# The last expert's rows added from their row buffer, gathered rows by diagonal products, fillers at the entry

## The reference

```python
# hier_moe, cut
gate = softmax(top_v) * g_w                  # two experts of 32 for each token, with a weight each
def block(args):                             # rows of one expert
    tids, e, w = args
    xb = x_pad[tids]
    hdn = silu(xb @ w1[e]) * (xb @ w3[e])
    return (hdn @ w2[e]) * w[:, None]
out = segment_sum(y, slot_tok)               # each token adds its two rows
# after it, in both layers
x = layer_norm(DN_ALPHA * x + f, ln2_g[i], ln2_b[i])
```

## Time and profile before

| | |
|---|---|
| median of 3 runs | 2996.56 us (2993.69 to 2999.35) |
| profiled execution | 2994.94 us, span 2993.1 us |
| mean granted TensorE clock | 0.982 |
| TensorE busy | 2895.8 us, 97% of the span |
| VectorE busy | 2123.5 us, 71% |
| ScalarE busy | 1604.9 us, 54% |
| GpSimd busy | 358.4 us, 12% |
| memory read | 574.15 MB |

### The profile page before, as it was taken

The page is one execution under the profiler, slowest core; times in us unless marked ns, Lnnn a source line. Parts: engine busy times, 40 slices in busy tenths (PEclk is TensorE's granted clock), DMA queues, the critical chain, the costliest instruction groups (busy, mean ns, idle before and its releaser), DMA issues.

```text
span 2993.1 us, 38811 instructions
## 1 busy us (share of the span) xinstructions
PE 2895.8 (97%) x14261; PEld 2257.0 (75%) x14261; DVE 2123.5 (71%) x2376; ACT 1604.9 (54%) x1969; POOL 358.4 (12%) x273
## 2 busy tenths in 40 slices
PE   8999899999989999899999999999999999999998
PEld 7668776767768767677677668888888887888886
DVE  3485799999972467899999865674776648676762
ACT  3573588888853464788888743433222226522211
POOL 0000212222220002122222220100000000000000
PEclk9999899999999998999999999999999999999999
DMA  7303799999962125899999844301232223232222
GB/s 273 136 1 113 261 389 405 409 398 400 405 223 85 39 99 226 334 399 398 404 399 406 332 106 99 66 20 64 92 102 95 99 85 99 92 111 93 91 94 84
DMA packets 170900, 600.50 MB, mean 201 GB/s; under 512 B 21697, under 2 KB 71025, under 8 KB 121363
## 3 DMA queue, kind: packets, MB, share of 16 engines
q1 hardware_dynamic: 140432, 541.22, 48.5%
q0 software_dynamic: 19840, 52.60, 4.9%
q10 hardware_dynamic: 10499, 4.91, 0.6%
HBM read 574.15 MB, written 40.37 MB: 205 GB/s over the span
## 4 chain that ended last, share of the span: by engine, by line
PE 73%; DMA 11%; DVE 7%; ACT 5%; issue 3%; POOL 1%; DVEq 0%; SPq 0%; ACTq 0%; POOLq 0%
PE bank L2074 14%; PE bank L2076 14%; PE bank L2075 14%; DMA ring<-w_gate 6%; PE bank L2512 4%; PE bank L2509 4%; DMA ring<-w_up 3%; PE bank L2086 3%; PE bank L2794 2%; PE bank L2528 2%; PE bank L2081 2%; PE bank L2082 2%; PE bank L2138 1%; PE bank L2139 1%; ACT ring_rounded L1479 1%
## 5 line engine op out<-in xcount | busy, mean ns | idle before, releaser
L3601 DVE TENSOR_TENSOR ring_rounded<-ring,big_rounded 128x2048 fp32r<-128x2048 f32 x252 | 567.6, 2288 | 32.0 <-ACT big_rounded L1479 31.0
L1479 ACT ACTIVATE big_rounded<-ring 128x2048 fp32r<-128x2048 f32 x252 | 481.9, 1916 | 44.2 <-DMA ring<-w_up 33.2
L3096 DVE TENSOR_TENSOR ring_rounded<-ring,ring_rounded 128x2048 fp32r<-128x2048 f32 (+2 forms) x118 | 261.4, 2255 | 329.8 <-ACT ring_rounded L1221 329.4
L1221 ACT ACTIVATE ring_rounded<-ring 128x2048 fp32r<-128x2048 f32 (+2 forms) x124 | 226.5, 1876 | 369.3 <-DMA ring<-ffn_w_down 150.1
L3601 DVE TENSOR_TENSOR ring_rounded<-ring,ring_rounded 128x2048 fp32r<-128x2048 f32 x128 | 292.4, 2288 | 43.5 <-ACT ring_rounded L1479 43.1
L1479 ACT ACTIVATE ring_rounded<-ring 128x2048 fp32r<-128x2048 f32 x128 | 245.0, 1917 | 96.5 <-DMA ring<-w_gate 95.5
L2074 PE MATMUL bank<-XT_rounded,ring_rounded 128*128 128x512 f32 (+1 forms) x792 | 295.8, 374 | 0.4 <-DVE XH_rounded L3149 0.4
L2076 PE MATMUL bank<-XT_rounded,ring_rounded 128*128 128x512 f32 (+1 forms) x792 | 292.9, 370 | 0.0
L2075 PE MATMUL bank<-XH_rounded,ring_rounded 128*128 128x512 f32 (+1 forms) x792 | 292.9, 370 | 0.0
L2512 PE MATMUL bank<-ring_rounded,big_rounded 128*128 128x512 f32 x960 | 265.7, 399 | 7.4 <-DVE ring_rounded L3601 6.9
L2075 PE MATMUL bank<-ring_rounded,XH_rounded 128*64 128x512 f32 (+2 forms) x608 | 239.6, 394 | 0.0
(11 more groups left out here) (525 smaller groups left out, 5527.1 us busy)
## 6 DMA issues: line engine op xcount, KB each, us to landing
ring<-w_up SPq DMA_DIRECT2D x128, 1024.0 KB, 9.8
ring<-w_down SPq DMA_DIRECT2D x128, 1024.0 KB, 7.7
ring<-w_gate SPq DMA_DIRECT2D x128, 1024.0 KB, 7.9
ring<-ffn_w_up SPq DMA_DIRECT2D x44, 1024.0 KB, 7.0
ring<-ret_gdn_w_in SPq DMA_DIRECT2D x8, 2048.0 KB, 13.1
ring<-ffn_w_down SPq DMA_DIRECT2D x8, 2048.0 KB, 7.7
expert_rows<-lnp POOLq DMA_DIRECT2D x1, 12288.0 KB, 40.3
ring<-odd_w_qkv SPq DMA_DIRECT2D x6, 2048.0 KB, 8.1
```

Source lines behind the costliest of these rows:

```text
L1221: act.activation(one_pass(hi(c)[:, ks, :]), raw(c)[:, ks, :], ACT.Copy).then_inc(rounded[c.pair], 1)
L1479: act.activation(one_pass(expert_hi(j)), expert_raw(j), ACT.Copy).then_inc(signal("half_rounded").sem, 1)
L3096: dve.tensor_tensor(one_pass(w), w, parts(hi(c)[:, ks, :]), ALU.subtract).then_inc(split[c.pair], 1)
L3601: dve.tensor_tensor(one_pass(expert_raw(j)), expert_raw(j), parts(expert_hi(j)), ALU.subtract).then_inc(signal("half_split").sem, 1)
```

## The change

1. The last expert's rows aren't stored in the table and gathered again. VectorE builds, for each tile of tokens, a mark matrix (128 tokens x 64 places) that holds the token's gate weight at its place in the last expert's list. TensorE turns the four of them into one bank, ScalarE copies the result (`last_T`), and TensorE multiplies it with the row buffer.
2. The gathered rows are no longer added by VectorE. For each tile and each of the two choices VectorE makes a diagonal matrix of the token weights (`shares`), and TensorE multiplies it with the gathered rows into the same two banks. VectorE then only adds the banks to X.
3. GpSimd's gathers wait for 15 stores of the odd half and not 16, and for the last products that use the space of their targets.
4. Eight small VectorE operations (`last_weights`) come behind `gate_weights`, in front of expert 2.
5. In both layers two fillers go ahead of `positions(l, 0)` and two ahead of `positions(l, 1)`. The fillers at the seam fall from 9 to 0 after layer 0 and from 24 to 4 after layer 1.

All operands of the new products are plain f32.

```diff
@@ -1085,14 +1091,16 @@
                         pool.wait_ge(full[1], base[1] + e + 1)
                         gather(e + 2)
                 scatter(EXPERTS - 2)
-                scatter(EXPERTS - 1)
 
             def from_experts(l):
 
                 pool.wait_ge(signal("slots_ready").sem, signal("slots_ready").next(pool))
                 for half in range(2):
-                    pool.wait_ge(signal(f"y_stored{half}").sem, 16 * (EXPERTS // 2) * (l + 1))
+                    pool.wait_ge(signal(f"y_stored{half}").sem, 16 * (EXPERTS // 2 - half) * (l + 1))
+                pool.wait_ge(full[3], U[f"moe{l}"][3] + EXPERTS)
                 for t in range(T):
+                    if t == 2:
+                        pool.wait_ge(full[6], U[f"moe{l}"][6] + EXPERTS)
                     for j, dst in enumerate((XH[:, t, :], M["YG"][:, t, :])):
                         pool.indirect_dma_start(
                             dst, None, expert_rows, bass.IndirectOffsetOnAxis(ap=gath[:, TOP_K * t + j:TOP_K * t + j + 1], axis=0),
...
-            def moments(t):
-
-                act.wait_ge(signal("x_combined").sem, signal("x_combined").next(act))
+            def moments(l, t):
+
+                u = U[f"combined{l}"][2 * t + 1]
+                act.wait_ge(drained[u.bank], u.n + 1)
                 act.activation(XH[:, t, :], X[:, t, :], ACT.Copy, accum_out=ssq[:, 16 + t:17 + t]).then_inc(act_done.sem, 1)
...
+
+            def marks_T(l):
+
+                u = U[f"last{l}"]
+                act.wait_ge(full[u.bank], u.n + 1)
+                act.activation(M["last_T"], ps(u)[0:NARROW, :], ACT.Copy).then_inc(drained[u.bank], 1)
...
                 experts(0)
+                marks_T(0)
                 for c in W["qkv"][0:1]:
                     round_chunk(c)
...
@@ -2311,6 +2328,31 @@
 
                 return lambda t, kk: ap[:, kk, t * P:(t + 1) * P]
 
+            def marks_T(l):
+
+                u = U[f"last{l}"]
+                pe.wait_ge(signal("last_marked").sem, signal("last_marked").next(pe, T * (TOP_K + 1)))
+                pe.wait_ge(drained[u.bank], u.n)
+                for t in range(T):
+                    ins = pe.transpose(ps(u)[0:NARROW, t * P:(t + 1) * P], M["last"][:, t, :], ident)
+                ins.then_inc(full[u.bank], 1)
+
+            def combine(l, t):
+                base, u = U[f"moe{l}"], U[f"last{l}"]
+                if t == 0:
+                    pe.wait_ge(drained[u.bank], u.n + 1)
+                    for b in (5, 6):
+                        pe.wait_ge(drained[b], base[b] + EXPERTS)
+                us = U[f"combined{l}"][2 * t:2 * t + 2]
+                for c, v in enumerate(us):
+                    pe.wait_ge(drained[v.bank], v.n)
+                    pe.matmul(ps(v)[:, :], M["last_T"][:, t * P:(t + 1) * P], M["YE"][0:NARROW, 1, c * BANK:(c + 1) * BANK], start=True, stop=False)
+                pe.wait_ge(signal(f"rows_back{t}").sem, 16 * TOP_K * (l + 1))
+                for c, v in enumerate(us):
+                    for j, rows in enumerate((XH, M["YG"])):
+                        ins = pe.matmul(ps(v)[:, :], M["shares"][:, t, j, :], rows[:, t, c * BANK:(c + 1) * BANK], start=False, stop=(j == 1))
+                    ins.then_inc(full[v.bank], 1)
...
@@ -2445,9 +2487,13 @@
                 turn_tile(normed, X, 3, "x_normed")
                 logits(l, 2)
                 logits(l, 3)
-                for q in range(2):
-                    positions(l, q)
-                    first_rows(l, q)
+                spare = (4, 6)[l]
+                keep_warm(Use(spare, U[f"moe{l}"][spare]), 2)
+                positions(l, 0)
+                first_rows(l, 0)
+                keep_warm(Use(spare, U[f"moe{l}"][spare]), 2)
+                positions(l, 1)
+                first_rows(l, 1)
...
@@ -2711,9 +2757,12 @@
                 experts(0)
             if on(5):
                 pe.wait_ge(drained[U["rel"][0].bank], U["rel"][0].n + 1)
+                marks_T(0)
                 for j in range(EARLY_BIAS):
                     rel_bias(j)
-                first_chunk_by_tile("qkv", "ln20_T", X, "x_normed", feature_rows(x_lo_T), 9)
+                for t in range(T):
+                    combine(0, t)
+                first_chunk_by_tile("qkv", "ln20_T", X, "x_normed", feature_rows(x_lo_T), 0)
...
@@ -2734,7 +2783,11 @@
             if on(6):
                 experts(1)
             if on(7):
-                first_chunk_by_tile("mix_in", "rms0_T", XH, "xh_ready", None, 24)
+                marks_T(1)
+                keep_warm(U["combined1"][0], 4)
+                for t in range(T):
+                    combine(1, t)
+                first_chunk_by_tile("mix_in", "rms0_T", XH, "xh_ready", None, 0)
...
                 bounds(l)
                 gate_weights(l)
+                last_weights(l)
                 stage(2, 0, down=False)
...
-
-            def combine(t):
-
-                dve.wait_ge(signal(f"rows_back{t}").sem, signal(f"rows_back{t}").next(dve, 16 * TOP_K))
-                x = X[:, t, :]
-                dve.scalar_tensor_tensor(x, XH[:, t, :], wts[:, t, 0:1], x, ALU.mult, ALU.add).then_inc(dve_done.sem, 1)
-                dve.wait_ge(dve_done.sem, dve_done.next(dve))
-                dve.scalar_tensor_tensor(x, M["YG"][:, t, :], wts[:, t, 1:2], x, ALU.mult, ALU.add).then_inc(signal("x_combined").sem, 1)
-                dve.wait_ge(signal("x_combined").sem, signal("x_combined").next(dve))
+                last_marks(l)
+
+            def last_weights(l):
+
+                at, w, match, place_at = grp, gw, keep, wtmp
+                dve.tensor_scalar(n_most, which, float(EXPERTS - 1), float(2 - EXPERTS), ALU.is_equal, ALU.mult).then_inc(dve_done.sem, 1)
+                done()
+                dve.tensor_scalar(n_most, n_most, float(EXPERTS - 1), None, ALU.add).then_inc(dve_done.sem, 1)
+                done()
+                dve.tensor_scalar(match, ek, n_most, None, ALU.is_equal).then_inc(dve_done.sem, 1)
+                done()
+                dve.scalar_tensor_tensor(place_at, pos2, 1.0, match, ALU.add, ALU.mult).then_inc(dve_done.sem, 1)
+                done()
+                dve.scalar_tensor_tensor(at, place_at[:, :, 0], -1.0, place_at[:, :, 1], ALU.add, ALU.add).then_inc(dve_done.sem, 1)
+                done()
+                dve.tensor_tensor(match, match, wts, ALU.mult).then_inc(dve_done.sem, 1)
+                done()
+                dve.tensor_tensor(w, match[:, :, 0], match[:, :, 1], ALU.add).then_inc(dve_done.sem, 1)
+                done()
+                dve.tensor_tensor(wts, wts, match, ALU.subtract).then_inc(dve_done.sem, 1)
+                done()
+
+            def last_marks(l):
+
+                for t in range(T):
+                    dve.tensor_scalar(M["last"][:, t, :], k("places")[:, 0:NARROW], grp[:, t:t + 1], gw[:, t:t + 1], ALU.is_equal, ALU.mult).then_inc(
+                        signal("last_marked").sem, 1)
+                for t in range(T):
+                    for j in range(TOP_K):
+                        dve.tensor_scalar(M["shares"][:, t, j, :], ident, wts[:, t, j:j + 1], None, ALU.mult).then_inc(signal("last_marked").sem, 1)
+
+            def combine(l, t):
+
+                for c in range(2):
+                    u = U[f"combined{l}"][2 * t + c]
+                    dve.wait_ge(full[u.bank], u.n + 1)
+                    x = X[:, t, c * BANK:(c + 1) * BANK]
+                    dve.tensor_tensor(x, x, ps(u)[:, :], ALU.add).then_inc(drained[u.bank], 1)
+                    dve.wait_ge(drained[u.bank], u.n + 1)
...
                 for j in range(EARLY_BIAS):
                     shifted(j)
                 rest_of_chunk(W["qkv"][0])
-                combine(0)
-                combine(1)
+                combine(0, 0)
+                combine(0, 1)
                 norm_tile(0, neg_mean[:, 0:1])
                 for t in range(T):
                     if t + 2 < T:
-                        combine(t + 2)
+                        combine(0, t + 2)
                     rest_of_tile("ln20_T", t, x_lo_T)
                     if t + 1 < T:
```

31 lines of the change are left out of this document (19 added, 12 removed).

## The result

The changed kernel takes 3014.86 us (median of 4 runs, 3014.23 to 3015.05) where the kernel before, beside it, takes 2995.12 us (4 runs, 2992.48 to 2999.35): ratio 1.0064, 95% interval 1.0051 to 1.0077. That is slower by 19 us. The forecast was 3000, with 2989 to 3010 as its range; the result lies above it. The profiled execution has a span of 3013.2 us against 2993.1: +20.1.

What follows compares the result with a forecast made beforehand. TensorE was taken as nearly always busy, with the DMA engines also full in the expert loops and TensorE alone full between. Seam 0 +9.6, seam 1 -0.3, entries -5.8 sum to +3.5 on 2996.56: 3000, range 2989 to 3010.

Steps and rivals of the forecast that it cites:

- Entry fillers, -4.5 a layer: Entry: fillers hold the full clock level, `first_rows` records cost 0.112 us, expert 0 begins 4.5 us earlier a layer.
- The sentences on the Trainium skill: Entry: the load rule without clock term would make a series 6.8 us, winning 2 and not 8.4; trace disagrees.
- Rival (a): Entry: fillers don't hold the clock level, costing 6.4 us a layer; 3019 in all, chance 0.1.
- last_weights, +1.6 a layer: Before expert 2's `hidden`: eight small VectorE operations take 1.64 us, of which 1.6 a layer passes on.
- Seam 0, +11.2 and -1.6: After layer 0: combine on TensorE delays the first product 11.2 us; full clock level for eight products saves 1.6.
- rival (b): Seams dearer: low level at both first products (+3.2), entry gain only 4.0; 3004, or 3006 with waits; chance 0.3.
- Seam 1, +1.0 and -1.6: After layer 1: first product 1.0 us later, full level saves 1.6, a wait of some 0.3; net -0.3.
- The removed round trip: Seams: without the last store the gathers wait for an earlier one and start 5.8 us earlier; seam 0 gains nothing.
- rival (d): Gathers still start late behind other DMA transfers; seam 0 doesn't notice, seam 1 loses 2 us; 3002, chance 0.05.
- would lose some 2 us: Seam 1: without the gathers starting 5.8 us earlier, this seam would lose some 2 us more.
- The seams' +9.3: Both seams together: net +9.6 us after layer 0 and -0.3 after layer 1.
- the entries' -5.8: Both entries together: -4.5 from fillers and +1.6 from small operations, -2.9 us a layer, -5.8 in all.

Runs made afterwards that it cites:

- e7: Changed kernel without the sixteen diagonal products a layer; gathered rows are fetched and waited for but not added; ratio 1.0038.
- e3: Changed kernel with `first_rows` reading its weight operand with neighbouring elements, not 16 bytes apart; expert 0's output is wrong; 3006.89 us.
- e2: Kernel before with only the four entry fillers a layer added; 3000.60 us, ratio 1.0019.
- e4: Kernel before with the eight small VectorE operations of `last_weights` three times over, 24 a layer; 3005.43 us, ratio 1.0037.
- e9: Changed kernel with the first 2 MB chunk of the next weights held until the last stores of expert rows have landed; 3019.09 us.
- e1: Changed kernel without its four entry fillers a layer; 3008.66 us, ratio 1.0054.
- e8: Changed kernel with marked products kept, VectorE adding the gathered rows, no entry fillers, and other seam filler counts; 3001.04 us, ratio 1.0025.
- e5: Kernel before with `first_rows` reading neighbouring elements and expert 0's gate and up weights loaded in matching row order, no fillers; 2992.78 us.

## Why the prediction was wrong, step by step

*Entry fillers, -4.5 a layer: wrong, this is the step that failed.* It said that a record of `first_rows` costs about what the 128-column f32 record costs at the full level, 0.112 us, since "the two are alike". They are alike in type and size and not in how the weight operand lies in memory. Strided, a record takes 0.24 us at either level (the changed kernel's stretches, e7); with neighbouring elements it takes 0.12 at the full level (e3). Nothing was to be had from the clock, and the fillers' time was simply added, +6.0 in each entry. In the time this one term was forecast at -9 for both layers and cost +6 (e2, 3 to 9): 15 us apart, as much as 3015 is from 3000. I priced an operation by a row of another line, although the trace of before had this operation's own rows: 32 records in 7.78 us, the first of them while the clock was still falling. I read that length as the effect of the low level. Its first records, taken apart, would have told.

The sentences on the Trainium skill went wrong in the same place. The rule of "TensorE: Matmul & The Clock Gate", LDWEIGHTS, by which a weight load takes its columns over 1.2 GHz and has no clock term, was set aside by the row of L2323. For the line at issue the loads stayed at 308 to 331 ns over both levels (e7), so that they had no term for the clock is borne out there. For neighbouring elements it is not: L2323's loads took 192 ns and at the low level up to 333. The rule's size is borne out in neither: by it a load of 128 columns takes 0.107 us. The prediction also counted two loads a record, while the trace has one (128 loads and 128 products on L2429). With one, the rule as it stands gives an estimate of 3.4 us for a series at either level, and nothing for fillers to win; the series took 7.78, and the stride had to be known as well.

*Rival (a), 3019, chance 0.1* is nearest to what happened: the second pair ran at 1.2 GHz (3.67 us, 3.5 forecast) and pushed the marks. But its condition was wrong. It was to decide by the level at the second pair, as if held fillers gained; yet the series takes 7.78 us at either level, so fillers at the full level only cost less. In e7 the first pair ran at the full level (the second took 2.98 us), and the entry was still 3.4 us longer than before. So this rival's number came near 3015 partly by luck. With chance 0.1 the mechanism was priced too low: I had noted against it that the 36-column products kept the level, which in the changed kernel they did not to their end (4.07 us and not 3.66; in e3 and e7 they did).

*last_weights, +1.6 a layer: right.* 1.66 us in the trace; e4 puts the passing on at some 1.9 a layer, with 1.2 to 2.5 as its bounds, if it scales with the number of operations.

*Seam 0, +11.2 and -1.6: right, and in part by luck.* +11.04, but marks 0.5 and combine 1.1 us too cheap were offset by rel_bias 1.7 us too dear. The turn of tile 3 is +12.64 where the first product is +14.08, so -1.4 for the level. The low level of rival (b) came at neither seam: the first records took 0.47 us. That combine bounds this seam, with no wait for rows, is shown by the chain and by e7.

*Seam 1, +1.0 and -1.6: mis-sized.* +3.42 and -1.7. The terms: the marks 0.8 (0.5), the four fillers 6.0 at a granted clock of 0.59 (5.0), combine 22.07 (21.05). Per product that last one is 0.92 us and not 0.877.

*The removed round trip, "5.8 us earlier": wrong in size, right in effect.* 1.9 us of it came at seam 0 and 1.0 at seam 1, since the store now lands behind the 2 MB load (e9); this was rival (d). That seam 0 does not notice was right. That seam 1 "would lose some 2 us" by it is not borne out: no product of its combine waited for rows in the profile after.

*Sum.* Fillers 6 (e2), small operations 4 (e4, a third), diagonal products 9 (e1 against e8), and 4 for what e8 has left beside the small operations: 23, against 19 measured, each with some 3 us of uncertainty. The seams' +9.3 stands (+11.3 in the trace); the entries' -5.8 should have been some +10 (fillers 6, small operations 4). Left open: the last 0.4 us of the table hide shifts of -1.7 and +2 between turn 3 at seam 1 (+18.0) and the end, which no run took apart.

## What to carry to other kernels

Before you price a faster clock or a better cover for an operation, find a row of that very operation at the other level, even if it is only its first records: a look-alike may differ in how its operand is read. A stage that is shortened is worth what the next wait leaves (5.5 us became 1.0 and 2.4 here, and nothing that the time shows), so find that wait first. A cover that costs time of its own has to be priced as if it gained nothing: here it cost 3 to 9 us. And before a round trip is removed to start transfers earlier, see what the DMA queues carry in that moment, and whether anything waits for the rows first.

## What the runs showed of the hardware

- Loading a weight operand whose f32 elements lie 16 bytes apart takes 308 to 331 ns for 128 x 128 at either clock level, 0.24 us a record in a series (e7, the changed kernel). With neighbouring elements it takes 186 to 192 ns at the full level, 0.12 us a record, and up to 338 at the low one (e3, e5). So the clock pays for the second and not for the first.
- A strided series neither held nor raised the clock level. In the changed kernel and in e7 it fell from full to low within both series of layer 0, and in the kernel before it stayed at 0.50 through both. In e5, with neighbours and no fillers, it rose from 0.50 to 1.00 near 304.6. But neighbours don't always hold it: in e3 it stayed at 1.00 through the first series (3.81 us) and fell within the second (5.44 us). What decides this no run shows.
- After each expert loop TensorE stands 3.2 to 4.8 us with no wait that the profile shows (3.25 in the chain above) while the next weight load is in the queues; with the load held it is 0.6 to 1.0 us. In e9, TensorE then stood 3.17 us in the middle of `rel_bias`, after the load had begun. The profile lists a DMA queue for instructions (q8, 88 packets); whether TensorE waits there for its own instructions behind the load, no run shows.
- A 64-row and a 128-row f32 product of 512 columns take the same time (589 and 592 ns of a record at the full level, lines 2349 and 2353 of the changed kernel), so narrow marks save nothing.
